# Products of constants in TensorE's queue, in the two recurrence stages of a two-block network

## The reference

```python
kk = jnp.einsum('bhnid,bhnjd->bhnij', kb, k) * decay
sol = lax.linalg.triangular_solve(kk, rhs, left_side=True, lower=True, unit_diagonal=True)
...
y_diag = jnp.einsum('bnijg,bnijgr,bnjgrp->bnigrp', cb, seg, dtc[..., None] * xc)
...
def step(S, inp):                       # RWKV-7
    sa = jnp.einsum('bhij,bhj->bhi', S, a_t)
    S = S * w_t[:, :, None, :] + sa[..., None] * b_t[:, :, None, :] + v_t[..., None] * k_t[:, :, None, :]
    return S, jnp.einsum('bhij,bhj->bhi', S, r_t)
```

## Time and profile before

| | us |
|---|---|
| median of 3 runs (lowest to highest) | 3045.97 (3044.67 to 3046.77) |
| the profiled execution's own time | 3043.37 |
| its span, first to last instruction | 3041.6 |
| TensorE busy in the span | 2741.9 (90%) |
| VectorE, ScalarE, GpSimd busy | 1189.7, 517.5, 531.2 |
| mean granted TensorE clock | 0.928 of full |

### The profile page before, as it was taken

The page is one execution under the profiler, slowest core; times in us unless marked ns, Lnnn a source line. Parts: engine busy times, 40 slices in busy tenths (PEclk is TensorE's granted clock), DMA queues, the critical chain, the costliest instruction groups (busy, mean ns, idle before and its releaser), DMA issues. The chain is left out here.

```text
span 3041.6 us, 45357 instructions
## 1 busy us (share of the span) xinstructions
PE 2741.9 (90%) x20202; PEld 2017.3 (66%) x20202; DVE 1189.7 (39%) x1791; ACT 517.5 (17%) x983; POOL 531.2 (17%) x304
## 2 busy tenths in 40 slices
PE   6999888977899997997888788999989998899997
PEld 4556577753688885443766646888854454688886
DVE  2221233443699944103565524442120062444312
ACT  3222112220211101013443301000010062100001
POOL 0000244520000000000222103344400000343331
PEclk9999867998899998998887888999989999899998
DMA  6222100020222123111000001222213100122220
GB/s 267 111 111 87 53 2 2 2 84 28 74 93 83 59 77 114 55 69 56 3 2 2 3 28 56 87 102 89 83 57 111 59 25 28 56 83 83 84 83 28
DMA packets 16210, 196.29 MB, mean 65 GB/s; under 512 B 1768, under 2 KB 1896, under 8 KB 4112
## 3 DMA queue, kind: packets, MB, share of 16 engines
q1 hardware_dynamic: 16016, 193.39, 16.8%
HBM read 191.27 MB, written 2.12 MB: 64 GB/s over the span
## 5 line engine op out<-in xcount | busy, mean ns | idle before, releaser
L2807 PE MATMUL psum<-arena,weight_ring 128*128 128x256 f32 x3072 | 674.6, 381 | 14.0 <-PEq L1607 14.0
L2807 PEld LDWEIGHTS psum<-arena,weight_ring 128*128 128x128 f32 x3072 | 587.7, 191 | 95.5 <-issue 14.5
L226 PE MATMUL psum<-arena,weight_ring 128*128 128x512 f32 x1024 | 450.7, 602 | 52.3 <-PEq L1474 26.1
L226 PEld LDWEIGHTS psum<-arena,weight_ring 128*128 128x128 f32 x1024 | 197.5, 194 | 302.2 <-issue 285.7
L1754 PE MATMUL psum<-arena,weight_ring 128*128 128x256 f32 x1584 | 349.3, 382 | 11.1 <-PEq L1607 7.0
L1754 PEld LDWEIGHTS psum<-arena,weight_ring 128*128 128x128 f32 x1584 | 303.5, 192 | 53.7 <-issue 11.7
L468 PE MATMUL psum<-arena,weight_ring 128*128 128x512 f32 (+1 forms) x672 | 248.2, 529 | 2.7 <-ACT arena L601 2.7
L2181 POOL TENSOR_TENSOR arena<-arena,consts_sb 128x512 f32<-128x512 f32 x48 | 64.5, 1350 | 1003.5 <-ACT arena L2473 775.4
L468 PEld LDWEIGHTS psum<-arena,weight_ring 128*128 128x128 f32 x672 | 128.2, 193 | 114.5 <-issue 106.4
L2855 POOL TENSOR_TENSOR arena<-weight_ring 128x1024 f32<-128x1024 f32 x32 | 77.0, 2407 | 548.5 <-issue 519.9
L2863 POOL TENSOR_TENSOR weight_ring<-arena,weight_ring 128x1024 f32<-128x1024 f32 x32 | 80.9, 2529 | 372.4 <-PE psum L2807 372.2
(11 more groups left out here) (410 smaller groups left out, 3397.9 us busy)
## 6 DMA issues: line engine op xcount, KB each, us to landing
weight_ring<-in_mlp_up SPq DMA_DIRECT2D x16, 2048.0 KB, 7.7
weight_ring<-in_mlp_down SPq DMA_DIRECT2D x16, 2048.0 KB, 7.7
weight_ring<-in_ada SPq DMA_DIRECT2D x12, 2048.0 KB, 13.0
weight_ring<-in_gate_up SPq DMA_DIRECT2D x11, 2048.0 KB, 7.6
weight_ring<-in_w_in SPq DMA_DIRECT2D x7, 2048.0 KB, 11.1
weight_ring<-in_w_o SPq DMA_DIRECT2D x4, 2048.0 KB, 7.8
weight_ring<-in_w_kv SPq DMA_DIRECT2D x4, 2048.0 KB, 8.0
weight_ring<-in_down_a SPq DMA_DIRECT2D x4, 1536.0 KB, 6.4
```

The source lines that it names most:

```text
L226: mm = pe.matmul(bank[:, 0:width], w[:, k, m * P:(m + 1) * P], rhs(k), start=(k == 0), stop=(k == kt - 1))
L2807: mm = pe.matmul(g.banks[i][:, pair * HALF:(pair + 1) * HALF], left[:, j, pair * P:(pair + 1) * P], right(j), start=first and j == 0, stop ...
```

## The change

A helper multiplies the identity by a constant (`scan`, 512 columns of ones and zeros) into a bank that is free at that point; nothing reads the result and no semaphore is set. Each call adds two LDWEIGHTS and two MATMUL records to TensorE's list, and nothing to any other engine.

```diff
+def keep_busy(pe, g, bank, cols):
+
+    pe.matmul(bank[:, 0:cols], g.c.ident, g.c.scan[:, 0:cols], start=True, stop=True)
@@ stage_mixers, tensor, ssd
                     elif kind == "ydiag":
+                        keep_busy(pe, g, bank, SEQ)
                         pe.wait_ge(s.m4, 2 * m + d + 1)
@@ stage_mixers, tensor
+                def idle_bank(it, cols):
+                    if it < 2:
+                        keep_busy(pe, g, g.banks[6], cols)
+
+                idle_bank(0, SEQ)
+                idle_bank(0, SEQ)
                 for it in range(NC + 2):
...
                     ssd(use)
+                    idle_bank(it, 256)
...
                     ssd(use + 1)
+                    idle_bank(it, 256)
...
                     ssd(use + 2)
+                    idle_bank(it, 256)
...
                     ssd(use + 3)
+                    idle_bank(it, 256)
...
                     ssd(use + 4)
+                    idle_bank(it, 256)
@@ stage_rwkv_mix, tensor
                     if on(b):
+                        keep_busy(pe, g, g.banks[3], 256)
                         level_x(b, 2)
...
                     if on(a):
+                        if a == 0 or on(b):
+                            keep_busy(pe, g, g.banks[4], SEQ)
                         raw_b(a)
...
                     if on(b):
                         level_products(b, 4)
+                        keep_busy(pe, g, g.banks[3], 256)
```

## The result

The median of four runs is 2996.22 us (2993.03 to 2997.39), against 3045.66 (3044.67 to 3046.77) for four of the kernel before on the same chip: a ratio of 0.9836 [0.9819, 0.9853], 49.4 us less. The forecast was 3013, 33 us less. The sign and the mechanism were right, and the time lies in the range; the size was one and a half times the forecast's.

What follows compares the result with a forecast made beforehand. TensorE's work, partly at half clock, and waits for VectorE bound the kernel; -8.4 - 1 - 10 - 1 - 2 - 4 - 6 = -32.4 us from 3043.4 gave 3011, forecast as 3013 against the median 3046.0, range 2988 to 3039.

Steps and rivals of the forecast that it cites:

- rival 4: Second stage: VectorE becomes the bound, new waits take a third of the gain, 3020 us; chance 0.58 together with the forecast.
- `raw_b`, forecast -10: Second stage: calls of 512 ahead of `raw_b` end half its falls, -10 us, bounds 0 and -20.
- half: Second stage, `raw_b`: 20 us if no round falls; 2.0 us stay idle behind the call, so half taken, -10.
- `turn`, forecast -8.4: Second stage, rounds 4 to 7: the call of 256 ahead of `turn` ends the falls behind it, -8.4 us.
- A third of the wait filled should end it: Second stage, `turn`: the call leaves 0.96 of 1.41 us idle, which should end the fall, -8.4 us.
- the first and last rounds: Second stage, costs and ends: paid calls in rounds 1, 2 and 8 against -2 from shorter half-clock stretches, together -1 us.
- First stage up to 437 us, start included, forecast -6: First stage: start -2 us, rounds 0 to 2 net -4 us, the latter with bounds -20 and +8.
- I take a third: First stage, rounds 0 to 2: of at most 26 us that can return, a third does, -9 us.
- the +5 of costs: First stage, rounds 0 to 2: calls at unwaited "ydiag" and about six of 256 are paid, +5 us.
- After 437 us, forecast -6: First stage's later part: half of the three half-clock stretches' cost returns, net -6 us, bounds 0 and -13.
- As for `raw_b`, half: First stage after 437 us: "ydiag" waits filled by 0.9 us; half of 13 us returns, -6.5 us.
- Rival 1: Both stages: the calls hold the clock nearly everywhere, -59 us, 2987 us; chance 0.15.

Runs made afterwards that it cites:

- Experiment 1: The change without its calls in the second recurrence stage, so only the first stage's calls: 3024.71 us, ratio 0.9935 to the kernel before.
- experiment 6: The change without the `raw_b` calls: 3004.51 us; with these as the second stage's only calls: 3002.59 us; with them doubled: 2997.50 us.
- Experiment 7: The change without the ten 256-column calls in first-stage rounds 0 and 1: 3017.07 us; without the eight at "ydiag" uses instead: 2995.40 us.
- experiment 8: The change plus more calls at two "ydiag" uses, `turn` and the last `turn_back`: 2984.49 us; with further calls behind `stage_mix` and `feature_norm`: 2975.24 us.

## Why the prediction was right or wrong

**Right: what bounds the stages.** The waits belong to VectorE, the busy stretches to TensorE's clock, and the calls act on the second through the first. The sections of the second stage that a VectorE wait ends did not move: `lora` to `level_x(b, 2)` is 9.26 us before and after, `level_x(b, 3)` to `raw_b` 4.09 and 4.10. So the calls there are hidden, as costed, and rival 4 did not take its third.

**`raw_b`, forecast -10: mis-sized, -17.0 in rounds 2 to 7.** To `level_x(b, 4)` the rounds 3 to 7 took 8.76, 8.79, 7.92, 8.78 and 7.93 us and now take 4.92 four times and 6.35; round 2 gives 0.9 more. The target of 4.7 us was good, down to the mask, which VectorE has ready 2.63 us after `raw_b` starts, where 2.6 was estimated. But the new wait for it that was announced didn't come in these rounds: TensorE's products between are done only after 2.78 us, when `raw_k` starts. What failed is the "half", drawn from the two smaller waits (1.78 and 1.41 us). It took the length of the idle time left behind the call, 1.90 us, for what decides. Experiment 1 shows a wait of 2.94 us without a fall, and in experiment 6 the fall behind `raw_b` is shorter with calls placed elsewhere alone. So the wait's length doesn't decide by itself; that the calls at three places worked on one another is the likely reading, and what decides stays open.

**`turn`, forecast -8.4: -6.2.** Rounds 5, 6 and 7 gave 1.6, 2.8 and 1.6 us, and round 4 kept its fall (15.50 to 15.31). "A third of the wait filled should end it" held in three of the four rounds. Round 7 has no `lora` behind it; from its `level_x(b, 4)` to the next round's first `level_x` it takes 15.32 us instead of 16.91. The fall shows in the `level_x` behind `turn`, before and after:

```profile
1706.39 1.73 PE L2284 MATMUL psum<-arena 64*64 64x64 f32 x32 [0.26 <-DVE arena L2650]
1661.03 1.15 PE L2301 MATMUL psum<-arena 64*64 64x64 f32 x32 [0.26 <-DVE arena L2671]
```

`level_x(b, 2)`: -1.5 against -1. The stage: -27.3 against -21, so 2.6 us are left for `raw_b` in round 1 (1.5) and for the first and last rounds, which were put at -1 net.

**First stage up to 437 us, start included, forecast -6: -20.6.** This is the largest miss, and at its lower bound. Two parts were wrong. "I take a third", because the chain of a level would set the pace and a wait of 3.16 us filled by 0.9 would mostly fall anyway: the clock was 0.96 instead, so nearly all of the half-clock time went. And the +5 of costs was charged to calls ahead of no wait as if they bought nothing. Experiment 7 shows the ten of 256, which hold most of these, to be the ones that earn: without them 10.8 us are lost. The start was right in kind: line 1054 takes 1.40 us instead of 1.98 and the clock is full from there, though it took calls of the full size (with all calls in the 32x32 form of the same busy time line 1054 took 1.97 us and round 0 23.6, against 15.4).

**After 437 us, forecast -6: -1.4.** Right in mechanism, wrong in the term: the "ydiag" at 438.28 still waits 1.35 us and 17 us at half clock follow it. The stretch is in the windows above. Of the three stretches of before in this part, 10.2, 6.7 and 13.5 us, the first became the one of 17.0, the second went and the third became one of 6.7. The eight calls bring nothing net (experiment 7); with a second one at two uses the stage was shorter (experiment 8). In the kernel without the `raw_b` call the same code took 6.2 us less, all of it in this part, so -1.4 carries that much chance. "As for `raw_b`, half" carried a share from one place to another, and the two answered in opposite ways.

**Sum.** Second stage 6 us better than forecast, first 10 better; with -32.4 of the forecast that is -49, and the profiled executions differ by 47.9. Rival 1 (2987), with the clock held nearly everywhere, was nearer to the size in the second stage's `raw_b` and the first rounds, and wrong behind 437 us. None of the four large terms came out within 2 us: two were put too low, by 7.0 and 14.6 us, and two too high, by 2.2 and 4.6. That these offset each other in part is luck, and so is some of the total's place in the range.

By the Trainium skill ("TensorE: Matmul & The Clock Gate", Terms) half of the throttled time is lost. Over the whole kernel the mean clocks 0.928 and 0.950 make 438 and 299 us at half clock: 139 us less, for 48 us of span. That is 34%, below the 41% of one round's rows and well below the page's half. The calls themselves, by the forecast's price some 28 us at full clock and partly on the path, are a likely reason, and VectorE's waits, which don't shrink, another; no run parts the two.

## What to carry to other kernels

Where the mean granted clock of a busy stage is well below 1 and its half-clock stretches begin behind short waits of TensorE, wide products of constants with the full array size, placed into those waits and into the lightly loaded rounds ahead of them, are worth trying; an engine that is late anyway hides them. Judge them by the stage's length and mean clock, not wait by wait: take out groups of calls, since one group's gain shows up at another's place. Product groups that start behind a norm are the next place to look.

## What the runs showed of the hardware

- A fall of the clock is not settled by the wait in front of it: the same 2.94 us were followed by full clock in one round and by half clock in others of the same program, and a stage that started 20 us earlier fell in other rounds with the same total (359.4 us against 359.7).
- Size counts along both sides of the product. At equal busy time (433 and 420 ns a record) a 32x32 stationary part holds the clock less well than 128x128, and a call of 16 or 32 columns with 128x128 still keeps half the gain. What exactly counts stays open, as does the 13 us of the smallest form.
- The same code differs by 6 us from one kernel to the next. The first stage, identical in the change and in the kernel without the `raw_b` call, took 283.0 and 276.8 us; the fall in round 2 was 17 us long in one and 7 in the other, and later ones differ too. In experiment 1 it took 282.7 us with its falls in other rounds. Differences below that between two single profiles of such stages mean nothing without the runs' interval.
